# A hybrid decoder step: seven more mixer-A key blocks fetched during the prompt attention, mixer B's pages in turned order, and the top-k marking parted around two decode logits

## The reference

```
x <- LN0(alpha*x + 0.5*SwiGLU1(x))
h = x @ w_in                       # split among the heads
  mixer A: 12 heads, dilated causal windows (128,1),(512,4),(2048,16)
  mixer B: 4 query heads, 1 K/V head, top-k keys by an indexer's scores
x <- LN1(alpha*x + concat(o_A, o_B) @ w_out)
x <- LN2(alpha*x + 0.5*SwiGLU2(x))
x <- x + (p @ ple_proj) * sigmoid(x @ ple_gate)
```

## Time and profile before

| | us |
|---|---|
| median of 3 runs (lowest, highest) | 1467.94 (1467.0, 1468.16) |
| time of the profiled execution | 1468.33 |
| its span in the profile | 1466.7 |
| TensorE busy in the span | 1375.8 (94%) |
| VectorE busy in the span | 551.8 (38%) |
| mean DMA rate over the span | 184 GB/s |

### The profile page before, as it was taken

How to read it: one execution, slowest core, us unless ns; L and a number is a source line. 1 busy time by engine, 2 the same in 40 slices (tenths; PEclk the granted TensorE clock), 3 DMA queues, 4 the chain that set the end, 5 groups by cost and what they waited for, 6 DMA issues and landing times.

```text
span 1466.7 us, 30734 instructions
## 1 busy us (share of the span) xinstructions
PE 1375.8 (94%) x12059; PEld 1269.4 (87%) x12059; DVE 551.8 (38%) x1340; ACT 449.5 (31%) x833; POOL 627.5 (43%) x431
## 2 busy tenths in 40 slices
PE   6999999999989999997877897989999999999988
PEld 6999999999979988965555565979999999999888
DVE  5222222200242246777899524162222222110454
ACT  2122222211262333246644431153222222111441
POOL 6343333455465645321455003544333333554642
PEclk9999999999989999999999998989999999999999
DMA  6298755766355533331199898434565657665221
GB/s 231 86 269 316 257 197 208 250 230 213 124 180 170 157 87 102 137 103 53 41 277 283 259 319 312 137 133 167 192 208 192 215 192 269 213 222 173 70 70 47
DMA packets 95775, 269.83 MB, mean 184 GB/s; under 512 B 36306, under 2 KB 36691, under 8 KB 95161
## 3 DMA queue, kind: packets, MB, share of 16 engines
q1 hardware_dynamic: 89000, 255.34, 52.0%
q0 software_dynamic: 5632, 10.50, 2.6%
q10 hardware_dynamic: 1040, 2.62, 1.2%
HBM read 259.78 MB, written 109.10 MB: 252 GB/s over the span
## 4 chain that ended last, share of the span: by engine, by line
PE 81%; DVE 8%; POOL 4%; ACT 2%; issue 2%; DMA 2%; SPq 1%; ACTq 0%; DVEq 0%; POOLq 0%
PE bank L1615 22%; PE bank L1619 21%; PE bank L1617 21%; POOL w_rest L576 2%; DVE idx_scores L1457 2%; DMA cache_a_ring<-in_cache_a 2%; PE bank L1663 1%; PE bank L2158 1%; PE bank L1975 1%; PE bank L1965 1%; PE bank L1665 1%; PE bank L1664 1%; PE bank L1987 1%; DVE idx_scores_left L1403 1%; POOL x_rest L586 1%
## 5 line engine op out<-in xcount | busy, mean ns | idle before, releaser
L576 POOL TENSOR_TENSOR w_rest<-w_raw,w_high 128x1024 fp32r<-128x1024 f32 (+2 forms) x159 | 410.3, 2581 | 596.4 <-ACT w_high L751 595.5
L751 ACT ACTIVATE w_high<-w_raw 128x1024 fp32r<-128x1024 f32 (+2 forms) x159 | 180.2, 1134 | 778.0 <-PE bank L1619 746.0
L1615 PE MATMUL bank<-x_high,w_high 128*128 128x272 f32 x1808 | 378.1, 290 | 13.1 <-POOL x_rest L586 11.7
L1619 PE MATMUL bank<-x_high,w_rest 128*128 128x272 f32 x1808 | 374.6, 289 | 0.0
L1617 PE MATMUL bank<-x_rest,w_high 128*128 128x272 f32 x1808 | 373.4, 288 | 0.0
L1615 PEld LDWEIGHTS bank<-x_high,w_high 128*128 128x128 f32 x1808 | 284.3, 189 | 21.4 <-issue 16.6
L1617 PEld LDWEIGHTS bank<-x_rest,w_high 128*128 128x128 f32 x1808 | 284.8, 189 | 0.0
L1619 PEld LDWEIGHTS bank<-x_high,w_rest 128*128 128x128 f32 x1808 | 282.8, 189 | 0.0
L1058 DVE SCALAR_TENSOR_TENSOR hidden<-silu_gate,bank 128x272 f32<-128x272 f32 x88 | 34.5, 434 | 389.3 <-ACT silu_gate L771 389.3
L1615 PE MATMUL bank<-hidden_high,w_high 128*128 128x272 f32 x616 | 127.7, 288 | 0.0
L1619 PE MATMUL bank<-hidden_high,w_rest 128*128 128x272 f32 x616 | 127.5, 288 | 0.0
(11 more groups left out here) (317 smaller groups left out, 1875.2 us busy)
## 6 DMA issues: line engine op xcount, KB each, us to landing
out_a_sample<-in_cache_a SPq DMA_DIRECT2D x73, 1344.0 KB
w_raw<-in_w_wi SPq DMA_DIRECT2D x88, 512.0 KB, 5.2
cache_a_ring<-in_cache_a SPq DMA_DIRECT2D x112, 384.0 KB, 4.8
w_raw<-in_w_wo SPq DMA_DIRECT2D x32, 704.0 KB, 5.3
w_raw<-in_w_w_in SPq DMA_DIRECT2D x26, 512.0 KB, 3.7
w_raw<-in_w_gate SPq DMA_DIRECT2D x8, 640.0 KB, 3.9
bias_toeplitz<-rev_bias POOLq DMA_DIRECT2D x32, 128.0 KB, 2.6
kv_b_pages<-in_cache_b POOLq DMA_DIRECT2D x64, 64.0 KB, 4.1
```

The lines of the kernel that those rows point to most:

```text
L576: nc.gpsimd.tensor_tensor(rest_part(u0, i, j)[:, 0:tiles, :], RAW[:, slot, 0:tiles, :], high_part(u0, i, j)[:, 0:tiles, :].bitcast(F32), A ...
L751: nc.scalar.activation(high_part(u0, i, j)[:, 0:tiles, :], RAW[:, slot, 0:tiles, :], ACT.Copy).then_inc(S["hi_ready"], 1)
L1615: mm(banks[n][:, 0:HALF], wh, xh[n], start=start, stop=False)
L1619: last = mm(banks[n][:, 0:HALF], wl, xh[n], start=False, stop=stop)
```

## The change: what it does

- `EARLY_EXTRA = 7`: key blocks 3 to 9 get buffers of their own in space that is free by then (`KX_LOW`, three blocks, over the projected index queries; `KX_HIGH`, four blocks, over the projected values), each with a semaphore. They are issued during the prompt attention: three right behind blocks 0 to 2, four behind the constant tables.
- Blocks 10 and 11 take the places of blocks 3 and 4: issued after the last transposes of the prompt attention. The ring of five slots now holds the other 49 blocks in turns; block n of 10 or more waits for the block whose slot it takes over. So block 12 waits for block 0, 13 for 1, 14 for 2, 15 for block 10 (the first block that has the slot before it), 16 for 11, and from 17 on five blocks back.
- SP's pages: three to two key blocks, 1 behind block 12, 3 by block 13, 4 by block 14, 6 by block 15, all 64 by block 54.
- The pages go in turned order, 36 to 101 first, then 102 to 127 and 0 to 35, which lie where the early blocks lie; POOL waits once for the tenth block's transposes before it goes on to page 103.
- Marking: 12 rounds before the logits of a = 2, 18 before those of a = 3, the last two rounds and the closing instruction behind them.
- The order of the value slots is turned so that the slot that is free first is taken first, as before.

```diff
+EARLY_RING, EARLY_EXTRA = 3, 7
+EARLY = EARLY_RING + EARLY_EXTRA
+N_RING = 56 - EARLY_EXTRA
+PAGES_FREE = (36, 102)
...
+        def key_turn(n):
+            return n if n < EARLY_RING else n - EARLY_EXTRA
+        def key_of_turn(r):
+            return r if r < EARLY_RING else r + EARLY_EXTRA
...
             def load_keys(n):
-                if n >= KEY_RING:
-                    sp.wait_ge(S["ka_t"], n - KEY_RING + 1)
-                sp.dma_start(AR[:, n % KEY_RING, :], cache_rows(n, 0)).then_inc(ar_in[n % KEY_RING], 16)
+                if n >= EARLY and key_turn(n) >= KEY_RING:
+                    sp.wait_ge(S["ka_t"], key_of_turn(key_turn(n) - KEY_RING) + 1)
+                landed, _ = key_landed(n)
+                sp.dma_start(key_block(n), cache_rows(n, 0)).then_inc(landed, 16)
...
-            for n in range(3):
+            for n in range(EARLY_RING):
+                load_keys(n)
+            sp.wait_ge(S["ix_relu"], 3 * IDX_HEADS)
+            sp.wait_ge(S["qblocks_done"], 1)
+            for n in range(EARLY_RING, EARLY_RING + 3):
                 load_keys(n)
             sp.wait_ge(S["lo_ready"], FIRST["w_out"])
             sp.dma_start(OHB[:], onehots[:, KEY_BLOCKS_A:24, :]).then_inc(S["oh_in"], 16)
             sp.dma_start(TOPC[:], consts[:, 356:740]).then_inc(S["topc_in"], 16)
+            sp.wait_ge(S["proj_out"], 48)
+            for n in range(EARLY_RING + 3, EARLY):
+                load_keys(n)
             sp.wait_ge(S["pt_ps"], 2 * N_STEPS)
-            for n in range(3, KEY_RING):
+            for n in range(EARLY, EARLY + KEY_RING - EARLY_RING):
                 load_keys(n)
...
-            for n in range(KEY_RING, 56):
+            for n in range(EARLY + KEY_RING - EARLY_RING, 56):
                 load_keys(n)
-                while page_at < min(64, (5 * (n - 4) + 3) // 4):
-                    load_kv_page(sp, 2 * page_at)
+                while page_at < min(64, 3 * (n - EARLY - 1) // 2):
+                    load_kv_page(sp, PAGE_ORDER[2 * page_at])
                     page_at += 1
...
-            for q in range(1, DEC_BATCH * PAGES, 2):
-                load_kv_page(pool, q)
+            for i in range(1, DEC_BATCH * PAGES, 2):
+                if i == PAGES_FREE[1] - PAGES_FREE[0] + 1:
+                    pool.wait_ge(S["ka_t"], EARLY)
+                load_kv_page(pool, PAGE_ORDER[i])
...
                 elif a == 2:
-                    mark_rounds(0, 32)
-                    v.tensor_scalar(SC[:], SC[:], PASSED_LIMIT, NEG, ALU.is_ge, ALU.mult).then_inc(S["topk_dec_done"], 1)
+                    mark_rounds(0, 12)
+                else:
+                    mark_rounds(12, 30)
                 dve.wait_ge(S["ka_sc"], 15 * (a + 1))
...
+            mark_rounds(30, 32)
+            v.tensor_scalar(SC[:], SC[:], PASSED_LIMIT, NEG, ALU.is_ge, ALU.mult).then_inc(S["topk_dec_done"], 1)
```

More of the change, by code:

```diff
@@ L70 @@
 KEY_RING, VALUE_RING = 5, 7
-VALUE_SLOTS = (1, 2, 3, 4, 0, 5, 6)
+VALUE_SLOTS = (4, 0, 1, 2, 3, 5, 6)
+EARLY_RING, EARLY_EXTRA = 3, 7
+EARLY = EARLY_RING + EARLY_EXTRA
+N_RING = 56 - EARLY_EXTRA
+PAGES_FREE = (36, 102)
 N_VALUE_STEPS = 32
@@ L231, in build_program @@
         KTA = sb("k_a_t", [128, 2, WIDTH_A], at=split_at + KEY_RING * WIDTH_A * 4)
+        KX_LOW = sb("k_a_early_low", [128, 3, WIDTH_A], at=h_at)
+        KX_HIGH = sb("k_a_early_high", [128, 4, WIDTH_A], at=h_at + C_VA * T * 4)
         KTB = sb("k_b_t", [128, 2, 512], at=e_at + 2208)
@@ L281, in build_program @@
         toe_in = [ctx.enter_context(nc.semaphore(f"toe_in{i}")) for i in range(4)]
+        early_in = [ctx.enter_context(nc.semaphore(f"early_in{i}")) for i in range(EARLY_EXTRA)]
         ar_in = [ctx.enter_context(nc.semaphore(f"ar_in{i}")) for i in range(VALUE_RING)]
@@ L392, in pt_copies @@
                     (PTA[0:32, q % 2, 7, :], bank[0:32, 384:512])]
+        PAGE_ORDER = list(range(PAGES_FREE[0], PAGES_FREE[1])) + list(range(PAGES_FREE[1], 128)) + list(range(PAGES_FREE[0]))
         def load_kv_page(eng, q):
@@ L404, in scores_done, with is_extra, key_block @@
             return n + 1 + n // 14
-        KEY_LOADS = [len(range(slot, 56, KEY_RING)) if slot < KEY_RING else 0 for slot in range(VALUE_RING)]
+        KEY_LOADS = [len(range(slot, N_RING, KEY_RING)) if slot < KEY_RING else 0 for slot in range(VALUE_RING)]
+        def key_turn(n):
+            return n if n < EARLY_RING else n - EARLY_EXTRA
+        def key_of_turn(r):
+            return r if r < EARLY_RING else r + EARLY_EXTRA
+        def is_extra(n):
+            return EARLY_RING <= n < EARLY
+        def key_block(n):
+            if not is_extra(n):
+                return AR[:, key_turn(n) % KEY_RING, :]
+            e = n - EARLY_RING
+            return KX_LOW[:, e, :] if e < 3 else KX_HIGH[:, e - 3, :]
         def key_landed(n):
-            return ar_in[n % KEY_RING], 16 * (n // KEY_RING + 1)
+            if is_extra(n):
+                return early_in[n - EARLY_RING], 16
+            return ar_in[key_turn(n) % KEY_RING], 16 * (key_turn(n) // KEY_RING + 1)
         def value_slot(m):
@@ L517, in load_values @@
                 elif slot < KEY_RING:
-                    sp.wait_ge(S["ka_t"], 56 - (55 - slot) % KEY_RING)
+                    sp.wait_ge(S["ka_t"], key_of_turn(N_RING - 1 - (N_RING - 1 - slot) % KEY_RING) + 1)
                 else:
@@ L527, in _ @@
             sp.dma_start(TOPC[:], consts[:, 356:740]).then_inc(S["topc_in"], 16)
+            sp.wait_ge(S["proj_out"], 48)
+            for n in range(EARLY_RING + 3, EARLY):
+                load_keys(n)
             sp.wait_ge(S["pt_ps"], 2 * N_STEPS)
-            for n in range(3, KEY_RING):
+            for n in range(EARLY, EARLY + KEY_RING - EARLY_RING):
                 load_keys(n)
-            sp.wait_ge(S["proj_out"], 48)
             sp.wait_ge(S["new_rows_out"], 16 * 2 * DEC_BATCH)
@@ L2032, in _ @@
                         last = tr(BANK[2 * (n % 2) + c // 4][:, 128 * (c % 4):128 * (c % 4) + 128],
-                                  AR[:, n % KEY_RING, 128 * c:128 * c + 128], IDENT)
+                                  key_block(n)[:, 128 * c:128 * c + 128], IDENT)
                     last.then_inc(S["ka_t"], 1)
```

## The result

| | before | changed |
|---|---|---|
| median of 22 runs each (lowest, highest) | 1468.7 (1465.02, 1475.25) | 1475.38 (1470.01, 1480.26) |
| ratio to before, 95% interval | | 1.0044 (1.0032 to 1.0056) |
| time and span of the profiled execution | 1468.33, span 1466.7 | 1479.93, span 1478.3 |

The changed kernel is slower by 0.44%, some 6.5 us (4.7 to 8.2 by the interval). The profiled execution of after is one of the longest of the 22, so the two spans differ by more than the kernels do.

What follows compares the result with a forecast made beforehand. SP's issuing of pages and keys was taken to pace the key stage; +3.0 (block 55's issue) + 2.0 (marks) - 0.2 = +4.8 us, giving 1473.1 for the profiled execution and 1472.7 for the median; range 1465.0 to 1476.5.

Steps and rivals of the forecast that it cites:

- the slow clock on the values: Rival, chance 0.08: longer idle before the first values drops TensorE's clock to 0.50, losing 2.4 us; time 1475.1.
- SP paces the key stage: Key stage: SP issues back to back, 1.14 us a page and 0.50 a key; two thirds of its time are pages.
- The gap at block 15: Key stage: SP stands 6 to 7 us before block 15's key until block 10 is transposed, its pages queued behind.
- Block 55's issue: Last key of the key stage: issued at 838.4, 3.0 us later than before; bounds 833.4 and 839.2.
- The irregular part: SP's long issues between block 15 and the last key: 5.8 us before, taken as 5.0, with 0 to 5.8 possible.
- the lower bound of 833.4: Earliest issue of block 55, if all of SP's irregular issue time came from fuller DMA engines and went away.
- Landing: End of key stage: block 55's transposes again begin 3.87 us after its issue, so the last scores move by +3.0.
- The marking: End of key stage: two marks and the closing instruction between the last logits and `pt_out(1)` cost 2.0 us.
- The gain foreseen as worth nothing: ScalarE's 3.16 us wait behind block 46 for the logits of a = 2 goes; worth 0, at most 0.8 us.
- The stop behind block 32: Key stage: TensorE still stands until 799 for the logits of a = 1, then catches up at 1.38 us a block.
- What was costed at nothing: Early blocks during prompt attention, POOL's bias loads and wait, turned pages, value slot order: no cost; 6.1 us landing covered.
- After the key stage: Value stretches: a late start is passed on whole, but for some tenths the fuller ring gives back; -0.2 us.

Runs made afterwards that it cites:

- half keys: The changed kernel with only 384 of 768 columns of each key block loaded, the issues and waits kept; 1475.56 in one execution.
- the two pairs: Kernel before and changed kernel, each profiled twice without further edits: spans 1466.7 and 1478.3 in the first pair, 1470.6 and 1476.5 in the second.

## Why the prediction was right, and by how much off

The forecast was 4.8 us more; 6.5 (4.7 to 8.2) was measured. The two terms that make up the forecast, SP's stand and the late marks, were the ones foreseen and came out near their sizes; a third, the slow clock on the values, had been set aside as a rival with a chance of 0.08 and belongs in the sum. Step by step:

- **SP paces the key stage**: right, and more plainly than the prediction could say: the 1.6 us of ring waits that it reads from the earlier trace rows as little are none at all. Halving the bytes left SP's 94 us where they were, while the same bytes on another queue took 7.5 us off the time.
- **The gap at block 15**: right. 737.7 to 744.66, where 737.6 to 744.9 was worked out; 6.9 us of ring wait in both profiles. The lists' totals of 11.0 and 9.9, instead of the 7 to 9 forecast, hold 4.1 and 3.0 us at other keys, whose slots were free. DMA share 0.42 in the gap (below 0.6 forecast) and 0.85 up to 808.
- **Block 55's issue**: 838.4 forecast, 838.45 measured; +3.0 against +3.24 and +3.38 counted from the first MAX8. The irregular part, 5.0 by choice, was 5.4 us (93.79 - 88.4); that it came out so near is luck, since the bounds were 0 and 5.8. The half keys, one execution, show as much of it at a lower load on the DMA engines, so nothing speaks for the lower bound of 833.4.
- **Landing**: taken as the same before and after, 3.87 us. It was 3.8 and 4.8 before, 4.7 and 5.3 changed: +0.8 and +0.5 in the two pairs. In the other kernels the same block took from 3.2 to 6.8 us (2.7 for half of it), and before's second profile, with 4.8, lies above the 4.3 under which it was to stay if the difference were the change's. So the spread from one execution to the next is enough to explain it; a share of the change isn't shown.
- **The marking**: right in its own 2.0 us: +2.0 at `pt_out(1)` (3.40 and 3.41 against 1.40 and 1.39), 2.02 forecast. What the longer stand does to the clock comes on top, see the last point. The gain foreseen as worth nothing is there too: ScalarE's exponential behind block 46 runs without a wait now, and the end doesn't come sooner.
- **The stop behind block 32**: right for this kernel (TensorE goes on at 798.75, 799 forecast) and right that it hides there; I did not see that it would be the bound as soon as SP is relieved.
- **What was costed at nothing**: POOL's bias loads and pages run at the times of before, and the prompt attention ends as it did. Landings there can be longer than the 6.1 us reckoned with, 12.9 us for the last of the early blocks; the bias loads, which the cover is for, landed in 3.1 us at the median against 2.6.
- **After the key stage**: -0.2 forecast; the pairs give +5.6 and -1.8 from the first value to the end, so nothing of that size can be read.
- **Slow clock on the values**: the term that the sum lacks. It was foreseen, from the idle piece of 0.85 + 2.0 us, priced at 2.4 us and given 0.08. It came in both profiles of the changed kernel and in all five with late marks, in none of the eight without, and cost 1.4 and 1.5 us up to the 384th value product.

By the table, the first value moved by these terms in the two pairs: issue 3.24 and 3.38, from there to the transposes 0.83 and 0.47, to the logits 0.12 and 0.40, to `pt_out(1)` 2.00 and 2.02, together 6.20 and 6.27 with the last hundredths. With the slow clock that is 7.6 and 7.8; without the second and third terms, which vary by as much between two executions of one kernel, 6.7 and 6.9. Both lie inside the interval of 4.7 to 8.2 around the measured 6.5. The first value product itself came at 850.26, where 849.3 was forecast. The 4.8 lies at the interval's lower end: what it lacks is the slow clock and some tenths of the issue.

## What to carry to other kernels

Before fetching earlier, ask which queue issues the fetches, and whether it stands for a free slot: a queue that hardly ever does, while its consumer waits, is itself the bound; fewer bytes do nothing for it, and a new wait in its list holds everything behind it. Time gained in one stretch must be spread over what the consumer still needs, since the last five of a row that come early come too late to be used. And work with room of its own ahead of a wait belongs there, not behind it: behind it, two marks cost their own 2.0 us and, by the longer stand of TensorE, some 1.5 us of slower products.

## What the runs showed of the hardware that was not expected

- A 384 KB block's landing on busy queues varies between places and executions: 3.8 and 4.8 us for the last block in two executions of the kernel before, 3.2 to 6.8 over all kernels, 6.1 to 7.5 for five issued within 3.5 us; half the block took 2.7.
- SP's irregular issue time (5 to 6 us in 94) did not follow the DMA load: 5.4 us at 243 GB/s and 6.1 at 166.
- The Trainium skill, "DMA: Bandwidth & Descriptors", section "Issuing engines are not separate DMA queues", has the start of a transfer cost its sequencer little beside the transfer. For one transfer that is so here too: 0.50 us of SP for a key that lands 4.6 us after its issue. But many of them in one list add up: the 1.64 us of a page and a key on SP set the pace of a stage whose DMA share was 0.95, and a share of 0.60 did not change it.
- TensorE went on at the lower clock (1.54 us for six transposes instead of 0.88, as in the earlier trace rows) behind idle pieces of 1.70 us in the kernel before, 2.98 in the changed one and 3.68 with pages on POOL in the kernel before; behind 1.92 ahead of the first value, in the changed kernel's second profile, the first 0.86 us still ran at the higher clock and the fall came behind them. Ahead of the values, the fall went with 1.92 to 2.98 us of idle time in five profiles of five, and with up to 0.89 us in none of eight.
